# A decoder layer in three-pass fp32: one new order on all engines, and the gate-times-up products on VectorE

## The reference

```
x = x + 0.5 * swiglu(rmsnorm(x, g_ffn1), w1_gate, w1_up, w1_down)
x = x + mix(rmsnorm(x, g_mix))             # causal pooling heads and a state-space mixer
x = x + cross_attn(rmsnorm(x, g_xq), ...)  # 4 heads over 256 memory rows
x = x + 0.5 * swiglu(rmsnorm(x, g_ffn2), w2_gate, w2_up, w2_down)
swiglu(h, g, u, d) = (silu(h @ g) * (h @ u)) @ d,   inner width 2816
```

## Time and profile before

| | us |
|---|---|
| median of 3 runs | 2313.57 |
| lowest, highest | 2311.26, 2315.73 |
| the profiled execution | 2313.38 |
| its span | 2311.5 |
| TensorE busy | 2237.8 (97%) |
| VectorE busy | 1385.5 (60%) |
| mean granted TensorE clock | 0.984 |

### The profile page before, as it was taken

The page is one execution under the profiler, slowest core; times in us unless marked ns, Lnnn a source line. Parts: engine busy times, 40 slices in busy tenths (PEclk is TensorE's granted clock), DMA queues, the critical chain, the costliest instruction groups (busy, mean ns, idle before and its releaser), DMA issues.

```text
span 2311.5 us, 41150 instructions
## 1 busy us (share of the span) xinstructions
PE 2237.8 (97%) x16044; PEld 2169.3 (94%) x16044; DVE 1385.5 (60%) x2575; ACT 680.4 (29%) x1106; POOL 295.7 (13%) x320
## 2 busy tenths in 40 slices
PE   7899999999999999999999999988999999999999
PEld 6899999999999999986899988988999999999988
DVE  5766565646666575455877335248656665466655
ACT  5322222222113232245624034123322222221212
POOL 2011010122212000012400000000101010131220
PEclk8899999999999999999999999999999999999999
DMA  4323223143223221147533334322313223152221
GB/s 167 96 79 97 68 64 101 55 173 121 83 102 98 76 57 39 37 148 229 196 109 122 128 109 151 126 74 67 105 56 97 68 66 99 58 199 84 101 74 76
DMA packets 222561, 234.38 MB, mean 101 GB/s; under 512 B 8963, under 2 KB 179729, under 8 KB 222185
## 3 DMA queue, kind: packets, MB, share of 16 engines
q1 hardware_dynamic: 222449, 232.83, 31.0%
HBM read 180.42 MB, written 52.48 MB: 101 GB/s over the span
## 4 chain that ended last, share of the span: by engine, by line
PE 56%; DVE 6%; issue 1%; ACT 1%; DMA 0%; POOL 0%; DVEq 0%; SPq 0%; ACTq 0%; POOLq 0%
PE bank L2919 17%; PE bank L2920 16%; PE bank L2921 16%; PE bank L3572 1%; PE bank L3584 1%; PE bank L3691 1%; DVE dec L2473 1%; PE bank L3604 1%; DVE cea L2485 1%; PE bank L3593 0%; PE bank L3626 0%; PE bank L3401 0%; PE bank L3614 0%; DMA w_raw<-in_w_down_dram 0%; DVE w_lo L1784 0%
## 5 line engine op out<-in xcount | busy, mean ns | idle before, releaser
L2919 PE MATMUL bank<-h_hi,w_hi 128*128 128x352 f32 (+1 forms) x3392 | 1057.6, 312 | 35.3 <-ACT p_gate L1258 16.4
L2920 PE MATMUL bank<-h_lo,w_hi 128*128 128x352 f32 (+1 forms) x3392 | 1046.8, 309 | 0.0
L2921 PE MATMUL bank<-h_hi,w_lo 128*128 128x352 f32 (+1 forms) x3392 | 1046.6, 309 | 0.0
L2919 PEld LDWEIGHTS bank<-h_hi,w_hi 128*128 128x128 f32 x3392 | 643.2, 190 | 41.6 <-DVE w_lo L1857 16.7
L2920 PEld LDWEIGHTS bank<-h_lo,w_hi 128*128 128x128 f32 x3392 | 644.1, 190 | 0.0
L2921 PEld LDWEIGHTS bank<-h_hi,w_lo 128*128 128x128 f32 x3392 | 642.8, 190 | 0.0
L2100 DVE SCALAR_TENSOR_TENSOR x<-bank,x 128x352 f32<-128x352 f32 x448 | 229.3, 522 | 144.3 <-PE bank L2921 144.2
L1857 DVE TENSOR_TENSOR w_lo<-w_raw,w_hi 128x1024 fp32r<-128x1024 f32 x120 | 154.7, 1303 | 70.2 <-ACT w_hi L1208 70.2
L2919 PE MATMUL bank<-xr,w_hi 128*128 128x264 f32 x640 | 181.5, 284 | 1.8 <-DVE p L1985 1.8
L2920 PE MATMUL bank<-xr,w_hi 128*128 128x264 f32 x640 | 181.8, 284 | 0.0
L2921 PE MATMUL bank<-xr,w_lo 128*128 128x264 f32 x640 | 181.5, 284 | 0.0
(11 more groups left out here) (405 smaller groups left out, 2856.3 us busy)
## 6 DMA issues: line engine op xcount, KB each, us to landing
act_keep<-act SPq DMA_DIRECT2D x88, 264.0 KB, 2.0
w_raw<-in_w_gate_dram SPq DMA_DIRECT2D x44, 512.0 KB, 5.3
w_raw<-in_w_up_dram SPq DMA_DIRECT2D x44, 512.0 KB, 6.0
w_raw<-in_w_down_dram SPq DMA_DIRECT2D x44, 512.0 KB, 3.5
h_raw<-act_keep SPq DMA_DIRECT2D x24, 528.0 KB, 4.6
l_raw<-act_keep SPq DMA_DIRECT2D x20, 528.0 KB, 5.3
w_raw<-in_w_in_dram SPq DMA_DIRECT2D x18, 512.0 KB, 4.4
x<-x_keep SPq DMA_DIRECT2D x6, 1408.0 KB, 10.2
```

The lines of the kernel that those rows point to most:

```text
L2919: eng.matmul(out, a_hi, b_hi, start=first, stop=False, skip_group_check=onto)
L2920: eng.matmul(out, a_hi, b_lo, start=False, stop=False, skip_group_check=onto)
L2921: return eng.matmul(out, a_lo, b_hi, start=False, stop=last, skip_group_check=onto)
```

## The change

All of it is order, but for one move of work to another engine.

- **Products.** `times` for chunks 1 to 10 moves from GpSimd's list to VectorE's, into `up_sums`, two behind each step. GpSimd keeps `low_mid`.
- **First chunk.** `take_p1(GATE)` of chunk 1 no longer waits for g_mix. On VectorE `plain_mult(5)` comes behind s2 low and ahead of the rest; s4 low is split off and comes later; the gate sums of chunk 1 are mixed with the up weights' lows. ScalarE's list is put in a like order.
- **Down projection.** The two lows of the next chunk's weights come behind adds 2 and 5 of the first column tile in place of behind the first and second tile; those of the last chunk come inside chunk 8, behind adds 1 and 4 of its third tile, in place of behind the loop.
- **last_split.** All three splits come ahead of weight units 2 and 3.
- **Start, first feed-forward.** SyncE keeps the first rows of x ahead of loads 3 to 5; TensorE turns tiles 4 to 8 of x between other pairs; even pairs go block by block with gate and up in turn; `x_split` runs two scales ahead of its lows; weight lows, evictions and squares change places (ScalarE's list too, not shown in full).
- **Entry, second feed-forward.** `norm_sum(4,1)` comes ahead of `norm_factors(4,0)`, `norm_stat(4,2)` and `norm_spread(4,2)` move by a part of a pair, ScalarE's `plain_hi(1,1)` comes ahead of `out_square(2)`.

```diff
             g_unit(0, 0, 2)
-            for t in (3, 4, 5):
-                xload(t)
 
             def keep_group(g):
 
@@ -734,6 +732,8 @@
                 keep(g, X_GROUPS[g][0] * P, min(b * P, T))
 
             keep_group(0)
+            for t in (3, 4, 5):
+                xload(t)
             g_unit(0, 0, 1)
             xload(6)
...
-            def times(f, c, j, t):
-
-                half, fi, step = ((1, 1, "22"), (1, 0, "21"), (0, 1, "12"))[j]
-                u_ = (p522[t][:, :], first_p[UP][:, t, :], wsum[:, t, :])[j]
-                out = quarter(act, half, fi, t)
-                eng.wait_ge(g_evict, evicted(f, c, "silu", GATE, j))
-                eng.wait_ge(g_mix, mixed(f, c, step, UP, t))
-                eng.tensor_tensor(out, u_, out, ALU.mult).then_inc(g_act, 1)
-
-            def multiply(f, c):
-
-                for j in range(3):
-                    for t in range(2):
-                        times(f, c, j, t)
-
-            def feed_forward(f):
-
-                eng.sem_inc(g_act, 6)
-                with eng.Fori(1, LAST) as i:
-                    multiply(f, i)
-                low_mid(f, 0, 0)
-                multiply(f, LAST)
-                low_mid(f, 1, 1)
+            def down_lows(f):
+
+                for c_ in range(2):
+                    low_mid(f, c_, c_)
                 with eng.Fori(0, 3) as j:
                     low_mid(f, 2 * j + 2, 0)
                     low_mid(f, 2 * j + 3, 1)
@@ -1035,7 +1016,7 @@
             eng.wait_ge(s_const, 5)
             x_stats(1)
             x_stats(2)
-            feed_forward(0)
+            down_lows(0)
...
             def take_p1(f, c, m, t):
 
                 n = chunks(f, c)
-                if m == GATE:
+                if m == UP:
+                    wait(eng, g_act, 6 * n)
+                elif not (isinstance(c, int) and c == 1):
                     wait(eng, g_mix, mixed(f, c, "21", GATE, 1) - len(MIX))
...
                     g_hi(f, 1, "A", m)
                 s2_split(f)
                 s4_split(f)
-                for kind in "DB":
-                    g_hi(f, 1, kind, GATE)
                 plain_act(f, 5)
-                take_p1(f, 1, GATE, 0)
+                for t in range(2):
+                    take_p1(f, 1, GATE, t)
                 s1_split(f)
-                take_p1(f, 1, GATE, 1)
+                g_hi(f, 1, "D", GATE)
+                g_hi(f, 1, "B", GATE)
+                take_p1(f, 1, UP, 0)
                 s3_split(f)
+                take_p1(f, 1, UP, 1)
                 for t in range(2):
                     silu_11(f, 1, t)
-                for t in range(2):
-                    take_p1(f, 1, UP, t)
                 g_hi(f, 1, "C", GATE)
                 for kind in "DBC":
...
 
                 hi_unit(U_IN, 0, 0)
                 hi_unit(U_IN, 1, 0)
-                split(0)
-                split(1)
+                for n in range(NT):
+                    split(n)
                 hi_unit(U_IN, 2, 0)
                 hi_unit(U_IN, 3, 0)
-                split(2)
...
             def x_split(f, n, between=None):
 
-                for k in range(KT + 1):
+                for k in range(KT + 2):
                     if k < KT:
                         x_scale(f, n, k)
-                    if k:
-                        x_low(f, n, k - 1)
+                    if k >= 2:
+                        x_low(f, n, k - 2)
                     if between is not None:
...
-            def s2_s4_low(f):
+            def s2_low(f):
 
                 eng.wait_ge(o_hi, 28 * f + 25)
                 eng.wait_ge(o_sum, 28 * f + 28)
                 eng.tensor_tensor(s2_lo[:, :, :], s2_f[:, :, :], s2_hi[:, :, :].bitcast(F32), ALU.subtract).then_inc(o_lo, 1)
-                eng.wait_ge(o_hi, 28 * f + 26)
-                eng.tensor_tensor(xr[:, KH:KT, 0:HT], x[:, KH:KT, 0:HT], xr[:, 0:KH, 0:HT].bitcast(F32), ALU.subtract)\
-                   .then_inc(o_lo, 1)
 
             def s1_low(f):
 
@@ -1917,6 +1890,12 @@
 
                 eng.wait_ge(o_hi, 28 * f + 28)
                 eng.tensor_tensor(xr[:, 0:KH, HT:T], x[:, 0:KH, HT:T], xr[:, KH:KT, HT:T].bitcast(F32), ALU.subtract)\
+                   .then_inc(o_lo, 1)
+
+            def s4_low(f):
+
+                eng.wait_ge(o_hi, 28 * f + 26)
+                eng.tensor_tensor(xr[:, KH:KT, 0:HT], x[:, KH:KT, 0:HT], xr[:, 0:KH, 0:HT].bitcast(F32), ALU.subtract)\
                    .then_inc(o_lo, 1)
...
+            def times(f, c, j, t):
+
+                half, fi, step = ((1, 1, "22"), (1, 0, "21"), (0, 1, "12"))[j]
+                u_ = (p522[t][:, :], first_p[UP][:, t, :], wsum[:, t, :])[j]
+                out = quarter(act, half, fi, t)
+                eng.wait_ge(g_evict, evicted(f, c, "silu", GATE, j))
+                eng.wait_ge(g_mix, mixed(f, c, step, UP, t))
+                eng.tensor_tensor(out, u_, out, ALU.mult).then_inc(g_act, 1)
+
             def gate_sums(f, c):
 
                 for step in (take_u, take_21, take_12):
@@ -2017,6 +2005,8 @@
                 for j, step in enumerate((take_u, take_21, take_12)):
                     for t in range(2):
                         step(f, c, UP, t)
+                    for t in range(2):
+                        times(f, c, j, t)
                     if j == 0 and between is not None:
                         between()
...
                 plain_mult(f, 3)
                 s1_s3(f)
+                s2_s4(f)
                 plain_mult(f, 4)
-                s2_s4(f)
                 for m in range(2):
                     g_low(f, 1, "A", m)
                     sums_13(f, 1, m)
+                s2_low(f)
+                plain_mult(f, 5)
                 sums_24(f, 1, GATE)
-                s2_s4_low(f)
+                s1_low(f)
                 for kind in "DB":
                     g_low(f, 1, kind, GATE)
-                plain_mult(f, 5)
-                s1_low(f)
                 s3_low(f)
                 for t in range(2):
                     act_11(f, 1, t)
                 g_low(f, 1, "C", GATE)
+                for t in range(2):
+                    take_w(f, 1, GATE, t)
+                s4_low(f)
                 sums_24(f, 1, UP)
                 for t in range(2):
-                    take_w(f, 1, GATE, t)
-                for kind in "DBC":
+                    take_u(f, 1, GATE, t)
+                for kind in "DB":
                     g_low(f, 1, kind, UP)
-                gate_sums(f, 1)
+                for t in range(2):
+                    take_21(f, 1, GATE, t)
+                g_low(f, 1, "C", UP)
+                for t in range(2):
+                    take_12(f, 1, GATE, t)
                 for m in range(2):
                     g_low(f, 2, "A", m)
...
             def down_chunk(f, c, parity):
 
+                first = isinstance(c, int) and c == 0
                 for n in range(NT):
-                    ffn_adds(f, c, n)
-                    if n < 2:
-                        down_low(f, c + 1, 1 - parity, n)
+                    for m in range(KT):
+                        ffn_add(f, c, n, m)
+                        if (n, m) in (((0, 7), (1, 7)) if first else ((0, 2), (0, 5))):
+                            down_low(f, c + 1, 1 - parity, n if first else m // 3)
+                        if isinstance(c, int) and c == LAST - 2 and (n, m) in ((2, 1), (2, 4)):
+                            down_low(f, LAST, 0, m // 3)
...
             def closing_loop(f):
 
-                with eng.Fori(0, 4) as j:
+                with eng.Fori(0, 3) as j:
                     down_chunk(f, 2 * j + 1, 1)
                     down_chunk(f, 2 * j + 2, 0)
-                for fi in range(2):
-                    down_low(f, LAST, 0, fi)
+                down_chunk(f, LAST - 3, 1)
+                down_chunk(f, LAST - 2, 0)
...
             x_stats(0)
-            x_evac(3)
+            for m in range(2):
+                plain_low(0, 0, m)
             x_factors(0)
             eng.sem_inc(g_sum, 8)
+            eng.sem_inc(g_act, 6)
+            x_split(0, 0, lambda k: x_evac(3) if k == 4 else None)
             for m in range(2):
-                plain_low(0, 0, m)
-            x_split(0, 0)
+                plain_low(0, 1, m)
             x_evac(4)
             x_evac(5)
-            for m in range(2):
-                plain_low(0, 1, m)
             plain_mult(0, 0)
             x_factors(1)
-            x_split(0, 1, lambda k: x_evac(6) if k == 3 else x_evac(7) if k == 6 else None)
-            plain_mult(0, 1)
-            x_evac(8)
-            plain_mult(0, 2)
+            x_evac(6)
+            x_split(0, 1, lambda k: x_evac(7) if k == 5 else plain_mult(0, 1) if k == 6 else x_evac(8) if k == 7 else None)
             x_factors(2)
-            x_split(0, 2)
+            x_split(0, 2, lambda k: plain_mult(0, 2) if k == 3 else None)
             first_chunk(0)
...
             add_out(16, 4, 1)
@@ -2825,6 +2820,7 @@
             norm_rs(4, 0)
```

(50 more changed lines are left out.)

59 lines of the change are left out of this document (25 added, 34 removed).

## The result

The changed kernel takes 2273.87 us in the median of 4 runs (2272.01 to 2275.62), against 2312.41 (2310.86 to 2315.73) for the kernel before beside it: ratio 0.9831, 95% interval 0.9814 to 0.9848. The forecast was 2273, with 2261 to 2292 around it. The profiled execution took 2272.01, with a span of 2270.3.

A forecast was written before the change was run, and what follows sets the result against it. TensorE, busy in 97% of the span, was taken as the bound, with a few long stalls and the half clock behind them to remove. Terms 9.8 + 15.0 + 6.3 + 10.4 - 0.8 = 40.7 off 2313.4 gave 2273 us, range 2261 to 2292.

The forecast's parts named there:

- start and first chunk, f = 0: First feed-forward's opening to (UP,6) of chunk 1: rearranged order gains 12.0 less a 2.2 dip, 9.8 us.
- down projections: Last weight pair's lows, both feed-forwards: loads land earlier, removing 11.0 of stall and two dips of 2.0, 15.0 us.
- split: Projection behind the first feed-forward: third split ahead of units 2 and 3 removes 3.7 and 2.6, 6.3 us.
- entry and first chunk, f = 1: Second feed-forward to (UP,6): 19.6 removed, less 2.5 small waits, 4.5 new wait and 2.2 dip, 10.4 us.
- closing chunks: Four products ahead of the last wsum cost at most 1.7 us each time; taken as 0.4 twice, -0.8.
- E: End of the third x_split; to move from 72.7 to 64.5 to 66.9 at the start, 6.7 earlier in feed-forward two.
- the new wait: At (UP,6) of chunk 1: chunk 2's up weights load after the later low of C; 4.5 us plus 2.2 dip.
- (b): The wait at (UP,6) stays hidden or causes no dip: 2 x 6.7 back, 2260 us; chance 0.13.
- (c): The start gains little, short waits leave half clock, the closing's 0.65 grows to a dip: 2283 to 2294; chance 0.15.
- (d): Waits only change name: last weight's lows still wait for their DMA, the split for adds: 2294 to 2309; chance 0.07.
- (e): Whole kernel: no change, all of the gain given back; chance 0.03.
- (f): VectorE bounds chunks 1 to 10, its 2.5 us on the path in all 20 chunks: slower, 2323; chance 0.02.

The follow-up runs named there:

- e5: Kernel before with only the places of down_low changed as in the change: 2295.3 us.
- e6: Kernel before with only last_split changed, ScalarE's third split ahead of weight units 2 and 3: 2306.3 us.
- e4: Changed kernel with ScalarE's two silu_11 of chunk 1, then the two take_p1(UP), ahead of s3_split: 2270.2 us.
- e9: Kernel before with only the start's new order, even pairs in turn in both feed-forwards: 2302.6 us.
- e2: Kernel before with only its products moved to VectorE: 2314.7 us.
- e1: Changed kernel with its six products a chunk back on GpSimd, the rest of the new order kept: 2270.3 us.
- e10: Changed kernel with the six products of chunk 10 behind all of its sums on VectorE: 2269.4 us.
- e12: Changed kernel with early up weights and silu_11 ahead of s3_split, all products on GpSimd, closing included: 2256.2 us.
- e11: Changed kernel with early up weights, silu_11 ahead of s3_split and closing products last, all products on VectorE: 2255.8 us.
- e3: Changed kernel with the low parts of chunk 1's up weights D, B and C earlier on VectorE: 2263.0 us.
- e7: Kernel before with only the first chunk's new order in both feed-forwards, products staying on GpSimd: 2307.0 us.
- e8: Kernel before with only norm_sum(4,1) ahead of norm_factors(4,0) at the second feed-forward's entry: 2302.9 us.

## Why the prediction was right

The total came out within 1 us. By the table of leads the terms are these:

| term | forecast | measured |
|---|---|---|
| start and first chunk, f = 0 | 9.8 | 14.3 |
| down projections | 15.0 | 7.8 + 7.2 = 15.0 |
| split | 6.3 | 6.5 |
| entry and first chunk, f = 1 | 10.4 | 10.0 |
| closing chunks | -0.8 | -1.1 - 1.6 = -2.7 |
| mixer, attention, last norm | none | -0.3 - 1.6 = -1.9 |
| sum | 40.7 | 41.2 |

The down projections and the split are right by their own mechanism. The entry is right in size, and one of its small waits has another cause. That the sum is right to 1 us is luck: the start gave 4.5 more than forecast, and the closings with what no term stood for took 3.8.

- **Down projection:** the forecast had the last pair's lows end near 713 on the kernel before's time, 1.2 us ahead of TensorE. They end at 700.10, which with the lead of 13.2 is 713.3. Right, and e5 alone shows it (15.1 in its trace).
- **Split:** e6 alone gives 6.1 by the medians and 6.5 in its trace. Right.
- **Second feed-forward's entry and first chunk:** the third `x_split` ends at 1558.0 in place of 1592.5; less the lead of 27.2 at the entry, E moved by 7.3 where 6.7 was said. The parts: 19.6 removed as said; the new wait and its dip 5.3 + 1.8 = 7.1 where 6.7 was said; small waits 4.2 (3.05, 0.7, 0.5) where 2.5 was said; 0.9 back, a wait for p L1985 that only the kernel before had. These make 9.2, and 0.8 stays open. The mechanism given for the small waits, VectorE's work behind E, is right for the last two only. The 3.05 is the count of g_evict (e4), which the forecast did not see although both lists were in the diff.
- **The start and the first chunk, f = 0:** the new wait and its dip are 4.3 + 2.7 where 4.5 + 2.2 was said. The step that was mis-sized is E, said to move from 72.7 to 64.5 to 66.9. It moved to 61.5. The forecast priced only single moves against each other, and charged 2 and 1.8 for turns of x in TensorE's path. It left out that the short waits in the first 60 us stood beside 17 us of half clock (the three windows at 0.50), and that this comes back with them. From the first product to chunk 1 it is 9.2 us, where TensorE had idled for 3.5; e9 shows it without any other part. How the rest divides between the clock and the new order of the work was not told apart. Also, the kernel before does not start alike each time: e2, e5 and e6, whose start is the old one, are 1.4 to 2.7 us ahead of it by chunk 10.
- **The closing:** the stall grew by 2 x 1.38, and in the second feed-forward 14 matmuls of 352 columns in 3.40 are 1.2 us over the 2.2 that they take at the full clock, so 4.0; the lead falls by 2.7, since the wait of 0.95 for a bank falls away. The forecast had both bounds, four products and the load of w_down behind them. The first, at most 1.7 each, was 1.38 and had been taken at 0.4; the second did bound, but only in part and in the second feed-forward. e1 and e10 show both: their stall is 0.65 again, and the load of w_down brings waits of 1.81 and 1.19 in their second closing.
- **The products in the steady chunks,** forecast at nothing: right, 41.0 us before and after, and e12 equals e11. VectorE's busy time in such a chunk rises by only 0.6 us, 24.64 to 25.22, with six instructions more: the interference that leaves gives back most of them. The Trainium skill ("GPSIMD Engine Reference", "Specifications") says that GpSimd shares its SBUF interfaces with VectorE and contends with instructions that have two SBUF inputs. The trace agrees, with 911 ns beside the products against 692 without.

The rivals: (b) did not happen, 4.3 and 5.3 us; e3 shows what it would have been worth, 10.9, near its 13.4. (c) was right in one half (a dip in a closing) and wrong in the other (the half clock of the start went). (d), (e) and (f) have nothing in their favour.

**What stays open.** The medians of e2 and e5 to e9 add up to 44.3 us of gain, and the whole change has 38.5. Two things in the traces point at the 5.8. From the entry of the second feed-forward to chunk 10, e7, e8 and e9 gain 3.4, 7.7 and 2.8 alone, 13.9, and the whole change 10.0: there they do not add, and the wait for the count is 1.6 in e7 and 3.05 in the whole. And the w_lo stall of the first feed-forward is 5.4 us in the kernel before's trace and 3.8 to 3.9 in those of e6, e8 and e9, which did not touch it. It is not a fixed price, and part of these three gains may be it. Neither was tried by itself.

## What to carry to other kernels

When instructions that count one semaphore change their order, check every wait on that semaphore: a position in a count can hold up work whose data has long been there. When a low or split step is moved back, follow the buffer that it frees to the load that waits for it, and from there to the first use; here that chain took 10.2 us and had been given 4.7. And compare a stretch of short waits by the same matmuls' starts, not wait by wait: here 3.5 us of waits stood in a stretch that gained 9.2. Last, a gain that is added up from medians is to be read beside the trace, stage by stage: e8's 9.4 held 7.7 of its own.
